# Recurrence kernel on one Trainium2 core: where the chain over the chunks stands among the other work of a step

## Reference

```
r, k, v, w_low, a_low, g_low = split(z + (z_prev - z) * mu)     # z = h @ w_in
w = exp(-exp(-softplus(-(w0 + tanh(w_low) @ w2)) - 0.5))
a = sigmoid(a0 + a_low @ a2)
kk = normalized per head (k * k_k);  k = k * (1 + (a - 1) * k_a)
for t in tokens:                       # per head, state 64 x 64
    sa = state @ (-kk[t])
    state = state * w[t] + outer(sa, kk[t] * a[t]) + outer(v[t], k[t])
    y[t] = state @ r[t]
y = group_norm(y) * lnx_w + lnx_b;  out = (y + bonus) * g
```

## Time and profile before

| | |
|---|---|
| median of 3 runs | 2833.71 us (2830.54 to 2837.58) |
| the profiled execution, its own time | 2839.56 us |
| its span | 2838.3 us |
| PE busy | 2568.9 us, 91% of the span |
| DVE busy | 1250.6 us, 44% |
| POOL busy | 931.9 us, 33% |
| ACT busy | 726.8 us, 26% |
| mean granted TensorE clock | 0.93 of full speed |
| first and last line 1574 (output of pair 0 and 7 copied) | 659.0 and 1011.2 us |

### The profile page before, as it was taken

One profiled execution on the slowest core, in us unless ns is written; L12 is line 12 of the kernel. 1 busy time (PEld: TensorE's weight loads), 2 busy tenths in 40 slices (PEclk: granted clock), 3 DMA queues, 4 the chain that ended last, 5 costly groups with the idle time before them and its releaser, 6 DMA issues.

```text
span 2838.3 us, 30081 instructions
## 1 busy us (share of the span) xinstructions
PE 2568.9 (91%) x12386; PEld 2046.6 (72%) x12386; DVE 1250.6 (44%) x1896; ACT 726.8 (26%) x949; POOL 931.9 (33%) x435
## 2 busy tenths in 40 slices
PE   6999898899999879889999978789999897899997
PEld 3777776767777667657888846668888676688886
DVE  3254444367777730176664235633331206433312
ACT  3211222233333232222222131122221232222212
POOL 4311221111111034334444433344444441444442
PEclk7998998699999889989999989899999998899998
DMA  5332231121111123313333311223333231233331
GB/s 201 110 94 67 74 89 45 53 56 32 44 41 37 37 75 91 91 52 97 97 97 107 86 45 56 82 68 99 96 110 96 67 97 30 67 97 97 110 92 50
DMA packets 428410, 222.34 MB, mean 78 GB/s; under 512 B 33823, under 2 KB 425842, under 8 KB 426994
## 3 DMA queue, kind: packets, MB, share of 16 engines
q1 hardware_dynamic: 403778, 208.28, 25.7%
q10 hardware_dynamic: 24496, 12.13, 1.5%
HBM read 214.61 MB, written 5.77 MB: 78 GB/s over the span
## 4 chain that ended last, share of the span: by engine, by line
PE 55%; DVE 4%; POOL 2%; ACT 2%; issue 1%; DVEq 0%
PE bank L306 55%; POOL w_low L302 1%; POOL h_low L507 1%; DVE sq L496 1%; PE bank L309 0%; ACT w_high L295 0%; ACT L468 0%; ACT h_high L517 0%; DVE ev_s L2076 0%; DVE ev_s L2078 0%; DVE sq L500 0%; DVE x_res L484 0%; DVE h_low L1808 0%; DVE rinv L460 0%; DVE h_high L1806 0%
## 5 line engine op out<-in xcount | busy, mean ns | idle before, releaser
L302 POOL TENSOR_TENSOR w_low<-w_raw,w_high 128x1024 fp32r<-128x1024 f32 (+1 forms) x331 | 861.9, 2606 | 1712.7 <-ACT w_high L295 1712.7
L306 PE MATMUL bank<-h_high,w_high 128*128 128x512 f32 x2008 | 834.3, 416 | 100.7 <-DVE h_low L507 42.5
L306 PE MATMUL bank<-h_low,w_high 128*128 128x512 f32 x2008 | 805.3, 401 | 0.0
L306 PE MATMUL bank<-h_high,w_low 128*128 128x512 f32 x2008 | 803.8, 400 | 0.0
L295 ACT CAST w_high<-w_raw 128x1024 fp32r<-128x1024 f32 (+1 forms) x331 | 359.9, 1088 | 1127.7 <-PE bank L306 1116.9
L306 PEld LDWEIGHTS bank<-h_high,w_high 128*128 128x128 f32 x2008 | 390.9, 195 | 225.0 <-issue 73.2
L306 PEld LDWEIGHTS bank<-h_high,w_low 128*128 128x128 f32 x2008 | 390.9, 195 | 85.9
L306 PEld LDWEIGHTS bank<-h_low,w_high 128*128 128x128 f32 x2008 | 392.5, 195 | 80.3 <-issue 4.9
L306 PE MATMUL bank<-g_high,w_high 128*128 128x512 f32 x352 | 139.1, 395 | 0.0
L306 PE MATMUL bank<-g_high,w_low 128*128 128x512 f32 x352 | 139.0, 395 | 0.0
L306 PE MATMUL bank<-g_low,w_high 128*128 128x512 f32 x352 | 139.0, 395 | 0.0
(11 more groups left out here) (314 smaller groups left out, 3198.3 us busy)
## 6 DMA issues: line engine op xcount, KB each, us to landing
w_raw<-in_w_in SPq DMA_DIRECT2D x58, 512.0 KB, 3.9
w_raw<-in_w_up SPq DMA_DIRECT2D x44, 512.0 KB, 3.8
w_raw<-in_w_ffn_gate SPq DMA_DIRECT2D x44, 512.0 KB, 3.8
w_raw<-in_w_ffn_up SPq DMA_DIRECT2D x44, 512.0 KB, 3.8
w_raw<-in_w_ffn_down SPq DMA_DIRECT2D x32, 704.0 KB, 4.5
w_raw<-in_w_ada SPq DMA_DIRECT2D x32, 512.0 KB, 3.9
w_raw<-in_w_down SPq DMA_DIRECT2D x16, 704.0 KB, 4.5
w_raw<-in_w_in ACTq DMA_DIRECT2D x21, 512.0 KB, 4.0
```

The lines of the kernel that those rows point to most:

```text
L302: self.G.tensor_tensor(self.w_low[:, slot, 0:k * P], self.raw_of(key)[:, 0:k * P], self.w_high[:, slot, 0:k * P].bitcast(F32), ALU.subtrac ...
L306: return self.T.matmul(out, lhsT, rhs, start=start, stop=stop, skip_group_check=True)
```

## The change

On PE the four groups of masked products now run without chain steps between them. Chain steps 1 to 5 come with the key's projection (one after each of K1 to K4, and step 5 behind step 4), `values_pe` follows, steps 6 and 7 come after R1 and R2, and the mean after step 7 (it stood after R1). On DVE all masks come first; then two chain steps go ahead of each piece of `block_dve`. Nothing is added or removed: each engine has the same instructions.

```diff
@@ recurrence_pe
             if has(i + 1):
                 self.arrive_pe(i + 1)
-                run(weave((self.keep_pe(i + 1), 1), (islice(chain, 4), 1)))
+                run(self.keep_pe(i + 1))
             if has(i + 2):
                 self.rank_pe(i + 2)
-            run(weave((some(self.projected_pe, i + 2, IN_K, 7), 1), (chain, 1)))
+            receptance = some(self.projected_pe, i + 2, IN_R, 6)
+            run(weave((some(self.projected_pe, i + 2, IN_K, 7), 1), (islice(chain, 5), 1)))
             if has(i + 1):
                 self.values_pe(i + 1)
-            receptance = some(self.projected_pe, i + 2, IN_R, 6)
-            next(receptance, None)
+            run(weave((islice(receptance, 2), 1), (chain, 1)))
             if has(i):
                 self.mean_pe(i)
-            next(receptance, None)
             next(receptance, None)
@@ recurrence_dve
                 self.arrive_dve(i + 1)
-                run(weave((self.keep_dve(i + 1), 1), (islice(chain, 4), 1)))
-            run(weave((some(self.block_dve, i + 1), 1), (chain, 1)))
+                run(self.keep_dve(i + 1))
+            run(weave((chain, 2), (some(self.block_dve, i + 1), 1)))
             if has(i):
                 self.closing_dve(i)
```

## The result

The changed kernel takes 2884.2 us (median of 5 runs, 2881.4 to 2887.4), the kernel before 2833.1 us (median of 5): a ratio of 1.0178 with a 95% interval of 1.0164 to 1.0192, 50 us slower. The forecast was 2876 us, with a range of 2860 to 2888.

A forecast was written before the change was run, and what follows sets the result against it. PE was taken to bound the kernel, busy 51.40 of 53.63 us a round. Six rounds losing 6.5 us each plus 3 us for round 6 made 42 us on the 2833.7 us median: 2876 us, range 2860 to 2888.

The forecast's parts named there:

- Masked products, steps 1 to 5: PE, round 2: K1 wins 1.5 us, spent again by uncovered step 5; values start about 765.2 against 765.01.
- Step 6 and the block pieces: Main term: step 6 behind values and R1, line 1360 at 769.2 instead of 762.37; PE idles 5.2 us before the mean.
- POOL beside line 1360: DVE's large block operation starts behind POOL's value-weight lowering and is held, ending 1.75 us later.
- Line 1109: DVE's key work becomes free of POOL, taking 0.49 instead of 2.62 us; gives 2.1 us back, line 1111 6.4 us late.
- Stage G: PE stage needing the inverses through memory: 8.28 us after line 1374, at 782.8, 6.6 us late.
- the bound of 10.25 us: Upper bound on time from line 1374 to stage G, from round 2, where G did not wait.
- The clock: PE's clock after idle time: no term in the main sum; a fall below 2.4 GHz was left to rival 2.
- Rival 2: Clock falls after PE's idle time, 1.5 us more a round, or transfers take longer: 52 us, 2886 us; chance 0.16.
- stage T's waits: Existing waits in PE's stage T, expected to take up some of the delay; 6.5 us a round taken.
- Round 6: No projection covers chain steps 1 to 4, and step 6 waits for the values: 1 to 4 us, 3 taken.
- Rival 1: No stall of line 1360 beside POOL: G 4.9 us late, 30 us in all, 2864 us; chance 0.18.
- Rival 3: Faster: output's copy under 2.1 us late, so line 1109's gain wins up to 2.2 us a round, 2819 us; chance 0.02.

The follow-up runs named there:

- the two last runs: Changed kernel with DVE's row cleared: 2838.8 us; the same plus POOL held behind the key's square and solving ahead of the scan on DVE: 2831.2 us.
- the early chain with the same two edits: Kernel before, with POOL's value-weight lowering held behind the key's square and, on DVE, solving ahead of the scan: 2823.6 us, ratio 0.9957.
- the last one: Changed kernel's chain places with DVE's row cleared, plus POOL held behind the key and solving ahead of the scan: 2831.2 us, ratio 0.9980.

## Why the prediction was right, and where it was off

*Masked products, steps 1 to 5.* Forecast for K1, step 4 and the values: 756.7, 763.8 and 765.2. Measured, with 11.85 us taken off: 756.7, 763.7 and 765.0. The waits for the masks, 0.54 us before group 3 and 0.21 us in `rank_pe`, are there.

*Step 6 and the block pieces.* Forecast 768.4 for step 6, 769.2 for line 1360, 774.5 for line 1374 and 775.5 for the mean; measured 768.3, 769.1, 774.4 and 775.4. The idle time was 4.97 us, against a forecast of 5.2. The run with DVE's order alone showed that this row is the cause.

*POOL beside line 1360.* Forecast 1.75 us, measured 2.81 - 1.04 = 1.77 us, in six rounds, which makes 10.6 us; the run with POOL held gained 12.5 us. The rows of 128 partitions carried over to 64. The Trainium skill ("SBUF — State Buffer", section "Who interferes with whom") says of VectorE's modes that use both of its SBUF ports that whoever issues first, VectorE or GpSimd, gets the shared pair of ports for the whole instruction, and that issue order decides who is blocked. The traces agree: line 1360 came 0.44 us behind POOL and was held, and in the run with the two-ahead order 0.02 us decided between 0.37 and 2.55 us for line 1374.

*Line 1109.* Forecast 0.49 us, measured 0.48. The copy came 8.4 us later than before and line 1111 6.3 us later, so the 2.1 us were given back as forecast.

*Stage G.* It did not wait for its transfers in rounds 1 to 6, which begin behind full rounds, with 8.3 to 9.4 us between line 1374 and G, so the bound of 10.25 us did not come in. The 8.28 us of round 7 is somewhat short of what a full round can need: in the run with POOL kept away and in the one with the idle time filled, one such G did wait (0.29 and 0.28 us), and began 8.6 us after line 1374.

*The clock.* This is the term that was too small: the sum put it at nothing. Rival 2 had the low clock behind the mean, but hidden up to R4, since it counted only the mean and R3 (some 4 us) and not the square, which also stands before the variance. The mean, R3 and the square took 1.09, 3.34 and 1.71 us in round 2, with granted clock 0.75 from step 7 to stage G and most of these matmuls at 1.2 GHz, and R4 came at 782.0 instead of the forecast 780.8. Where the clock rose early (round 3, variance 4.76 us after the mean) the round was 1.1 us shorter, and lost 6.5 us, just the forecast. Nor did stage T's waits take up anything: DVE was as late as PE, and the waits of 0.31 and 0.62 us stayed. Together a round lost 6.5 to 7.7 us, 7.1 us in the mean, instead of 6.5. That is 3.9 us of time over six rounds.

*Round 6.* Forecast 3 us out of 1 to 4, measured 4.4 us. Steps 2 to 4 stood alone, with waits of 1.11, 0.27 and 0.65 us. But the values began no later than before, counted from stage G (37.8 us behind it, and 38.5 before), so these waits are not the loss. What cost is that step 6 now stands behind the values, and these ran at the lower clock in both kernels (the first line is from the kernel before, the second from the changed one):

```profile
975.57 3.62 PE L306 MATMUL bank<-rw_v_tok,rw_keep 128*128 128x64 f32 x16
...
1014.76 3.62 PE L306 MATMUL bank<-rw_v_tok,rw_keep 128*128 128x64 f32 x16
```

Line 1360 then came 4.4 us later than before, counted from stage G, and with it line 1374 and the next G, which waited for its transfers in both. The prediction had this wait for the values but no price for them at the lower clock. So the stretches between stages G cost 47.3 us, not 42. The rest of the 50 us is in the scatter of the two medians.

*Rival 1* (no stall) fell with line 1360. *Rival 3* (faster) named the right condition, a copy less than 2.1 us late. With DVE's two-ahead order on the kernel before, the copy was 2.5 us late and the undisturbed rounds 0.3 to 0.6 us longer, which bears the give-back by line 1109 out. With the chain late and DVE's row cleared, the two last runs are about even with the kernel before, and the last is 6 to 8 us slower than the early chain with the same two edits.

## What to carry to other kernels

When steps of a chain between two engines are moved on one of them, read the other engine's row behind the last step: what stands there in order is added to the path, whatever it has to do with the chain. Then look what a third engine does at the new time, since an operation that starts just behind the other engine's can be held until that one ends: lines 1360, 1374, 1109 and 1588 all ended 0.2 to 0.9 us after POOL's lowering when they met it. The gain was not in the chain: two edits of order, POOL's work moved behind the key and the solving ahead of the scan, took most of PE's waits in a full round away and gave 0.43%.

## What was not expected of the hardware

- A race between DVE and POOL that 0.02 us decide: the same kernel took 2841 to 2865 us, and 2846 to 2849 us once the two operations were apart. A delay of 2.2 us in line 1374 cost 3.3 us a round, the rest by the clock.
- The clock fell with no long wait before it. In the run with steps 6 and 7 ahead of the values, the waits were 0.27, 1.16 and 0.27 us, with small products between them, and the values after them took 3.39 us. In four of the runs (POOL kept away, idle time filled, steps 6 and 7 ahead of the values, and the last one) it fell in one or two rounds at `rank_pe`, behind the masked products, where the waits are 0.54 and 0.21 us, and cost 1.6 to 3.2 us in such a round; in their other rounds, and in all full rounds of the changed kernel and of two more runs (only DVE's order changed; DVE's row cleared), with the same waits, it did not. What decides between them stays open.
- Why the kernel before did not show this in its profiled execution (full clock in all full rounds), though it has a wait of 0.52 us among the masked products, was not tried.
